# Token weight rows all loaded ahead, tiles' loads reordered, and wide exponentials in two pieces, in a hybrid decoder block on one Trainium2 core

## The reference, cut to what matters

```python
def hybrid_layer(x, mem, norm_g, w_in, ...):          # x: 2048 tokens of 1024, mem: 256 tokens
    h = rmsnorm(x, norm_g)
    proj = h @ w_in                                   # columns for the three head groups
    ...
    log_f = log_sigmoid(f_fg + b_forget)
    o_fox = fox_attention(f_q, f_k, f_v, log_f)       # 6 heads of 64
    ...
    mkv = rmsnorm(mem, mem_norm_g) @ w_mem_kv
    o_mem = memory_attention(m_q, mk, mv)
    return x + concatenate([o_gla, o_fox, o_mem]) @ w_out

def fox_attention(q, k, v, log_f):                    # per head, causal
    c = cumsum(log_f)
    s = q @ k.T * 64 ** -0.5 + c[:, None] - c[None, :]
    return softmax(where(causal, s, -inf)) @ v
```

## Time and profile before

| what | value |
|---|---|
| median of 3 runs | 1283.22 us (1281.21 to 1283.7) |
| the profiled execution | 1284.25 us, its span 1282.5 us |
| busy, share of the span | PE 1217.3 us (95%), DVE 659.4 (51%), ACT 544.5 (42%), POOL 414.7 (32%) |
| mean granted PE clock | 0.979 of full speed |
| PE busy in 0 to 41 us | 18.19 us |
| PE and DVE busy in 861 to 974 us (second round) | 107.00 and 97.06 us of 113 |

### The profile page before, as it was taken

The page is one execution under the profiler, slowest core; times in us unless marked ns, Lnnn a source line. Parts: engine busy times, 40 slices in busy tenths (PEclk is TensorE's granted clock), DMA queues, the critical chain, the costliest instruction groups (busy, mean ns, idle before and its releaser), DMA issues. The chain is left out here.

```text
span 1282.5 us, 18815 instructions
## 1 busy us (share of the span) xinstructions
PE 1217.3 (95%) x6256; PEld 996.9 (78%) x6256; DVE 659.4 (51%) x1494; ACT 544.5 (42%) x1106; POOL 414.7 (32%) x520
## 2 busy tenths in 40 slices
PE   5799999999999999998999979998999999799997
PEld 5799877888777777777888847876787787588886
DVE  4564434100333334432555358888898897544443
ACT  3453224012444443212555347786777777211111
POOL 6453641131333333322344143153136314211110
PEclk9799999999999999999999979999999999799999
DMA  7794223223333333435444494236044301533331
GB/s 259 244 311 156 70 76 109 80 82 107 106 107 106 106 106 122 129 120 168 132 148 130 133 212 136 69 99 157 9 147 99 86 10 36 212 148 148 148 141 73
DMA packets 106821, 161.57 MB, mean 126 GB/s; under 512 B 12149, under 2 KB 62325, under 8 KB 105125
## 3 DMA queue, kind: packets, MB, share of 16 engines
q1 hardware_dynamic: 103920, 151.46, 38.4%
q10 hardware_dynamic: 2616, 8.66, 1.7%
q0 software_dynamic: 192, 0.33, 0.2%
HBM read 102.67 MB, written 57.74 MB: 125 GB/s over the span
## 5 line engine op out<-in xcount | busy, mean ns | idle before, releaser
L1033 PE MATMUL tok_tps<-h_T,tok_slot 128*128 128x512 f32 x2088 | 491.2, 393 | 0.0
L1033 PEld LDWEIGHTS tok_tps<-h_T,tok_slot 128*128 128x128 f32 x2088 | 390.1, 188 | 83.3 <-issue 2.3
L2093 PE MATMUL out_yps<-out_w,out_mix 128*128 128x512 f32 x768 | 178.0, 394 | 8.4 <-POOL out_mix L2142 7.6
L2093 PEld LDWEIGHTS out_yps<-out_w,out_mix 128*128 128x128 f32 x768 | 145.9, 190 | 40.5 <-ACT out_w L2159 8.7
L1856 ACT ACTIVATE fox_pT<-fox_tps 128x512 fp32r<-128x512 f32 x240 | 124.1, 529 | 82.4 <-PE fox_tps L1790 78.4
L1912 DVE TENSOR_TENSOR fox_pT<-fox_tps,fox_pT 128x512 fp32r<-128x512 f32 x240 | 143.7, 606 | 20.3 <-ACT fox_pT L1856 18.3
L1901 DVE TENSOR_SCALAR_CACHE_REDUCE fox_prob<-fox_sps 128x512 f32<-128x512 f32 (+1 forms) x240 | 141.4, 604 | 13.8 <-PE fox_sps L1781 11.0
L1790 PE MATMUL fox_tps<-all_ident,fox_prob 128*128 128x128 f32 x816 | 132.8, 276 | 5.4 <-ACT fox_prob L1848 4.0
L1790 PEld LDWEIGHTS fox_tps<-all_ident,fox_prob 128*128 128x128 f32 x816 | 101.5, 141 | 32.7 <-ACT fox_prob L1848 7.4
L1848 ACT ACTIVATE fox_prob<-fox_prob,fox_nm 128x512 f32<-128x512 f32 (+7 forms) x96 | 114.8, 1196 | 6.0 <-POOL fox_kb L1563 5.6
L1803 PE MATMUL fox_ops<-fox_pT,fox_v 128*128 128x512 f32 (+3 forms) x384 | 112.2, 375 | 1.6 <-ACT fox_pT L1856 1.6
(11 more groups left out here) (199 smaller groups left out, 1667.4 us busy)
## 6 DMA issues: line engine op xcount, KB each, us to landing
scr_split<-cg_stage SPq DMA_DIRECT2D x64, 256.0 KB, 2.9
open_raw<-in_w_cols SPq DMA_DIRECT2D x22, 512.0 KB, 4.4
open_raw<-in_x SPq DMA_DIRECT2D x16, 512.0 KB, 7.1
tok_xT<-in_x_cols SPq DMA_DIRECT2D x16, 512.0 KB, 6.4
scr_gates<-cg_stage SPq DMA_DIRECT2D x32, 256.0 KB, 2.5
outw_mix<-scr_mix SPq DMA_DIRECT2D x16, 512.0 KB, 4.4
out_x<-in_x SPq DMA_DIRECT2D x16, 512.0 KB, 3.5
out<-out_o ACTq DMA_DIRECT2D x15, 512.0 KB, 2.6
```

Of the source, the lines that this page charges most:

```text
L1033: mm = nc.tensor.matmul(cps[u % 2], w[j % 2][a_][:, kk, :], hT[b_][:, kk, c * CH:(c + 1) * CH], start=(kk == 0 and r == 0), stop=(kk == KT ...
L2093: mm = nc.tensor.matmul(yps[t % 2][:, c, :], mix[t % 2][a][:, kk, :], w[b][:, kk, c * CH:(c + 1) * CH], start=(kk == 0 and n == 0), stop=( ...
```

## The change: what it does

- `RAW` goes from 4 to 8: each weight row has a tile of its own, and SP issues the eight loads without a wait. Rows 2 and 3 of x (as 128-token tiles) are loaded in `first_loads`, ahead of the stores of the memory keys; each waits for the squares of the tile that held its place.
- The high part of the weight rows moves from POOL (L359) to ACT (`round_weights`), between `squares` of tile 1 and the copy of the memory keys. POOL keeps the low part. Five rows (`EARLY`) are split in the memory block; the other three, `scale` of tile 1 and `rstds` of tile 2 move to the token block, and so do `squares` and `means` of tile 2.
- Tile 0 gets its high and low part in four pieces of two `kk` instead of two of four.
- The values of group 1 land on a semaphore of their own (`values_loaded`), which PE waits for at the weighing of key unit 4.
- Row tiles of turns 2 to 5 take their exponentials as keys 0 to 1023 and keys from 1024 on, each with a sum of its own. `plan` hands out at most one piece per key unit (two in turns of four units), and what is left behind the last unit. DVE adds the two sums ahead of the reciprocal and waits for its own addition.

```diff
@@ memory_keys_values, SP @@
-                sp.wait_ge(tokens.squared, 1)
-                tokens.load_rows(sp, 2)
-                sp.wait_ge(tokens.squared, 2)
-                tokens.load_rows(sp, 3)
                 sp.wait_ge(stored, 16 * 2 * MT)
@@ memory_keys_values, ACT @@
                 tokens.squares(act, 1)
+                for kk in range(KT):
+                    tokens.round_weights(act, kk)
                 act.wait_ge(k_done, MT)
                 nc.scalar.activation(kst[HI][:, :, :], kps[:, :, :], ACT.Copy).then_inc(ev_hi, 1)
-                tokens.squares(act, 2)
@@ memory_keys_values, POOL @@
-                for kk in range(KT):
+                for kk in range(tokens.EARLY):
                     tokens.split_weights(pool, kk)
-                    if kk in (1, 4):
-                        tokens.scale(pool, kk // 4)
-                    if kk in (2, 4):
-                        tokens.rstds(pool, kk // 4)
-                tokens.rstds(pool, 2)
+                    if kk == 1:
+                        tokens.scale(pool, 0)
+                    if kk == 2:
+                        tokens.rstds(pool, 0)
+                        tokens.rstds(pool, 1)
@@ TokenStage @@
-    RAW = 4
+    RAW = KT
     XT = 4
+    EARLY = 5
...
         for t in range(2, self.XT):
+            sp.wait_ge(self.squared, t - 1)
+            self.load_rows(sp, t)
             self.load_columns(sp, t)
 
+    def round_weights(self, act, kk):
+        act.wait_ge(self.w_loaded[kk], 16)
+        act.activation(self.w[HI][:, kk, :], self.w_raw[kk][:, :], ACT.Copy).then_inc(self.w_hi, 1)
+
@@ project_tokens, POOL @@
+                tk.split_weights(nc.gpsimd, tk.EARLY)
+                tk.scale(nc.gpsimd, 1)
+                for kk in range(tk.EARLY + 1, KT):
+                    tk.split_weights(nc.gpsimd, kk)
+                tk.rstds(nc.gpsimd, 2)
@@ forgetting_attention, plan @@
+            if ahead:
+                waiting = []
+                for m, (u, made, ready) in enumerate(out):
+                    waiting += [(i, piece) for i in ready for piece in pieces((t + 1) % n_turns)]
+                    n = len(waiting) if m + 1 == len(units) else min(len(waiting), 2 if len(units) < 2 * QT else 1)
+                    out[m], waiting = (u, made, waiting[:n]), waiting[n:]
             return ahead, out
+
+        def pieces(t):
+
+            return range(2 if turns[t % n_turns][1] >= 2 else 1)
@@ scores, PE @@
-                            pe.wait_ge(first.loaded[g], (r + 1 + n // n_scores) * 16 * Opening.LOADS)
+                            pe.wait_ge(first.loaded[g], (r + 1 + n // n_scores) * 16 * (Opening.LOADS - (g == 1)))
@@ exponentials, ACT @@
+                        cols = slice(0, w) if last == 0 else slice(0, 2 * CH) if piece == 0 else slice(2 * CH, w)
                         act.wait_ge(maxed, E.at(QT * t + QT - i))
...
+                        if piece == last:
+                            mm.then_inc(expd, 1)
@@ invert, DVE @@
+                        if len(pieces(t)) == 2:
+                            nc.vector.tensor_tensor(rsum[t % 2][:, 0, :], rsum[t % 2][:, 0, :], rsum[t % 2][:, 1, :], ALU.add
+                                                    ).then_inc(summed, 1)
+                            dve.wait_ge(summed, r * pieces_sum(n_turns) + pieces_sum(t + 1))
+                        nc.vector.reciprocal(rinv[t % 2][:, :], rsum[t % 2][:, 0, :]).then_inc(inverted, 1)
```

More of the change, by code:

```diff
@@ L234, in _ @@
                 tokens.normalise(dve, 0)
-                tokens.means(dve, 2)
             @block.gpsimd
@@ L327, in parts @@
     def parts(self, t):
-        return [slice(0, KT // 2), slice(KT // 2, KT)] if t == 0 else [slice(0, KT)]
+        return [slice(kk, kk + 2) for kk in range(0, KT, 2)] if t == 0 else [slice(0, KT)]
     def parts_before(self, t):
@@ L1538, in __init__ @@
         self.zeroed, self.filled = k.sem("zeroed"), k.sem("filled")
+        self.values_loaded = None if opening is None else k.sem("values_loaded")
         self.loaded = [k.sem("loaded")] if opening is None else (
@@ L1593, in load_values @@
     def load_values(self, eng, r, piece, c0, n=1):
-        self.send(eng, piece, self.values(c0, n),
-                  self.scr.fox_v[bass.ds(2 * r + self.e, 1), :, 4 * c0:4 * (c0 + n), :].rearrange("a p b c -> (a p) b c"))
+        done = self.values_loaded if self.opening is not None and piece == 1 else self.loaded[piece]
+        src = self.scr.fox_v[bass.ds(2 * r + self.e, 1), :, 4 * c0:4 * (c0 + n), :].rearrange("a p b c -> (a p) b c")
+        eng.dma_start(self.values(c0, n).bitcast(F32), src).then_inc(done, 16)
     def load_qk(self, eng, r, piece, c0, n=1):
@@ L1640, in forgetting_attention @@
         nm = [k.sb(f"nm{b}", [P, CH // P]) for b in range(2)]
-        rsum = [k.sb(f"rsum{b}", [P, CH // P]) for b in range(2)]
+        rsum = [k.sb(f"rsum{b}", [P, 2, CH // P]) for b in range(2)]
         rinv = [k.sb(f"rinv{b}", [P, CH // P]) for b in range(2)]
@@ L1680, in plan, with pieces_sum @@
                 done, tiles = upto, ready
+            if ahead:
[4 more added lines that the diff above has]
+                    out[m], waiting = (u, made, waiting[:n]), waiting[n:]
             return ahead, out
+        def pieces(t):
+            return range(2 if turns[t % n_turns][1] >= 2 else 1)
+        def pieces_sum(t):
+            return sum(len(pieces(i)) == 2 for i in range(t))
         def ends(t, m):
@@ L1843, in round_, with exponentials @@
                     K, G, E = Ring(r, n_keys), Ring(r, n_turns), Ring(r, QT * n_turns)
[L1845 to L1846 removed]
+                    def exponentials(t, i, piece):
+                        w, last = keys_of(turns[t % n_turns][1]) - (CH - P * (i + 1)), pieces(t)[-1]
+                        cols = slice(0, w) if last == 0 else slice(0, 2 * CH) if piece == 0 else slice(2 * CH, w)
                         act.wait_ge(maxed, E.at(QT * t + QT - i))
[L1848 to L1850 removed]
+                        mm = nc.scalar.activation(prob[t % 2][:, i, cols], prob[t % 2][:, i, cols], ACT.Exp,
+                                                  bias=nm[t % 2][:, i:i + 1], scale=-1.0,
+                                                  accum_out=rsum[t % 2][:, piece, i:i + 1])
+                        if piece == last:
+                            mm.then_inc(expd, 1)
                     def pt_high(u, n):
@@ L1875, in round_ @@
                             pt_high(u, k0 + m)
-                            for i in tiles:
-                                exponentials(t + 1, QT - 1 - i)
+                            for i, piece in tiles:
+                                exponentials(t + 1, QT - 1 - i, piece)
                             if ends(t, m):
```

32 lines of the change are left out of this document (13 added, 19 removed).

## The result

| | before | changed |
|---|---|---|
| median of the runs | 1283.07 us (1281.21 to 1283.7, 4 runs) | 1292.71 us (1290.72 to 1293.93, 4 runs) |
| ratio | | 1.0076, 95% interval 1.0058 to 1.0094 |
| the profiled execution | 1284.25 us, span 1282.5 | 1293.58 us, span 1291.8 |

A forecast was written before the change was run, and what follows sets the result against it. PE and DVE hand work to each other with ACT between, neither alone the bound. Terms -5.5 - 1.0 + 7.5 + 1.5 + 0 + 1.0 = +3.5 on 1284.25 give 1287.75, as median 1286.7 us; range 1277 to 1291.

The forecast's parts named there:

- the two sides: Whole kernel: gains of 5.5 and 1.0 us ahead of the rounds, against losses within the three rounds; net +3.5.
- Opening, -5.5: Memory block and tile 0: block ends at 31.5, first product 7.8 us earlier, less 2.3 for POOL holding DVE.
- The holds: Tile 0: DVE's quarters lengthened while POOL is busy; 2.3 us taken, half of at most 4.6.
- Entry, -1.0: Start of the forgetting block: values sent earlier, so PE's wait of 3.48 us shrinks by 1.0.
- End of turn 1, +2.5 a round: Three pieces left behind the last copy delay DVE's first negation by 2.5 us; 7.5 over three rounds.
- Ends of turns 2 to 4: ACT's chain longer by 0.29 us, DVE adds two sums (0.2): 0.5 a round at turn 2, later turns 0.
- Turn 2 in all, 0.5 a round and 1.0 for the clock, 2.5: Turn 2 over three rounds: 1.5 us for its longer end plus 1.0 for PE's slower clock.
- Clock, +1.0: Turn 2: PE's clock may halve after its stall ending turn 1; 1.0 us over three rounds, ends 0 and 4.5.
- the likeliest case: The forecast with its clock variant, slower than before: 1285.8 to 1291 us, chance 0.48.
- Turn 3, 0: End of turn 3: the copy of unit 13 comes 0.5 us earlier and frees PE; taken as 0.
- Turn 4, 0: End of turn 4: the copy of unit 13 comes 0.5 us earlier and frees PE; taken as 0.
- In the middle of a turn ACT waits for PE, so they cost nothing there: Mid-turn: 48 split exponentials add 13.9 us on ACT, but cost nothing where ACT waits for PE.

The follow-up runs named there:

- e1: Changed kernel with every exponential in one piece again and no sum on DVE; opening and values' own semaphore stay: 1272.25 us, ratio 0.9925.
- e2: e1 with the values of group 1 back on the common semaphore, so the opening alone: 1274.65 us, ratio 0.9942.
- e13: e1 with the exponentials of turn 1's last two row tiles held back behind the copy of the last key unit: 1281.61 us, ratio 0.9996.
- e5: e1 plus, ahead of the reciprocal of turns 2 to 5, the changed kernel's addition with a result nothing reads: 1281.83 us, ratio 1.0.
- e14: Changed kernel with the sum by TENSOR_REDUCE and no cap, both pieces where the whole exponential stood: 1278.31 us, ratio 0.9977.
- e3: Changed kernel with the two sums of a row added by one-operand TENSOR_REDUCE instead of two-operand TENSOR_TENSOR: 1285.87 us, ratio 1.003.

## Why the prediction was wrong, point by point

- *Right: the direction and the two sides.* A gain ahead of the rounds, a loss in each, and the end of turn 1 as a place of it. Both sides were too small, and the errors partly cancel: the gains were 4.7 us larger than forecast (8.25 and 2.95 for 5.5 and 1.0), the loss 10.8 us larger (20.8 for 10.0).
- *Opening, -5.5: too small, 8.25 in the trace, about 7.5 in the runs.* The block ended at 30.0 and not at 31.5, as landing took 2.5 to 3.2 us and not 5.5; the first product came 9.24 us earlier, not 7.8. The holds took most of what I had allowed at most: four quarters in 5.02 us, at 0.41 each without a hold, is 3.4 of the 4.6. The clock, which I had named as an end worth 2.6, was worth nothing (e1 beside the changed kernel), since tile 1 waits for DVE either way.
- *Entry, -1.0: too small, 2.95 by the trace of the changed kernel, 3.1 between the traces of e2 and e1, 2.4 between their medians.* The values' landing was nearly the whole of the wait. The upper end, 3.48, was the nearer one.
- *End of turn 1, +2.5 a round: 2.4 measured, not for that reason alone.* PE's wait was 2.95 us, where 3.3 was forecast. e13 gives 1.0 for a wait of 2.4 us in turn 1, without pieces or sum; e5 1.1 for the addition; e14 0.75 for the pieces; they overlap. That the size came out is in part luck, as the sum had no addition there.
- *Ends of turns 2 to 4, the step that failed.* "DVE adds two sums: 0.17 by the reciprocal's size, 0.2 with its own wait." A median of 0.905 us was measured, in twelve places, and it was on the path at the ends of turns 1, 2 and 3, where the sum had it at turn 2 alone. e5 prices the additions at 9.6 us, e3 at 5.9 beside the rest. I had the rule in hand in the opening, from the row of 1792 ns beside 677, and did not ask the same of an addition of 4 columns, because the row that I priced it by, the reciprocal, reads one operand. The Trainium skill, "GPSIMD Engine Reference", section "Specifications", says that GpSimd shares its SBUF interfaces with VectorE and contends with VectorE instructions that have two SBUF inputs; by that rule, the traces agree: TENSOR_TENSOR with two takes 0.16 us with POOL at rest and up to 1.17 beside it, TENSOR_REDUCE with one 0.15 to 0.16 beside it.
- *Turn 2 in all, 0.5 a round and 1.0 for the clock, 2.5: 9.5 measured*, the largest single miss. It holds the addition (0.9 to 1.0 a round by e5), the pieces (0.6 by e14), what is left of the late end of turn 1 (0.8 by e13) and the clock; these overlap.
- *Clock, +1.0: too small.* It fell in turn 2 of the changed kernel in all three rounds. At e13's price that is 4.5, the end that I had put outside the likeliest case, and the longer fall of the third round adds about 1 (22.93 against 21.97).
- *Turn 3, 0: +1.4 measured*, 1.1 of it the addition (e5) and 0.5 the pieces (e14). *Turn 4, 0*: +0.5 against the kernel before, +0.2 against e1, and turn 5 -0.6 and -0.3.
- *"In the middle of a turn ACT waits for PE, so they cost nothing there": held as far as shown.* In the second round of e14 no turn is longer by more than 0.1 but those at whose end the exponentials are waited for.

What stays open: how the held addition, the late end of turn 1 with its clock, and the pieces' fixed cost share the 6.7 to 7.6 us of a round, since removing two of them gave more than the sum; what decides whether the clock falls behind a given wait; and whether a microsecond is to be had with pieces in turns 4 and 5.

## What to carry to other kernels

Before an instruction is put between an engine's wait and the work that others wait for, look at what the neighbouring engine does at that moment: twelve additions of four columns cost here as much as everything else in the change gained. Price a new instruction by a row with the same kinds of operands, not the same number of elements; a sum over two values can be a reduction over one tile. And an exponential that is handed out later than it was belongs in the account of the next turn, with the clock that falls behind PE's wait.
